# A two-block float32 kernel on one core: earlier gelu and gate loads, narrow weight fetches, recurrence banks in the other order, aligned input rows

## The reference

```
x = first_block(x):                       # hybrid_layer, then rmsnorm
    z = rmsnorm(x) @ w_in                 # 7 parts of 1024 columns
    a recurrence over the tokens per head: r, i = sigmoid(block_diag(rnn_x)), h = a*h + u
    x += merged @ w_out; x += (silu(g)*u) @ w_down; x += gate * (p @ w_ple)
y = second_block(x):                      # hybrid_layer_2
    proj = rmsnorm(x) @ w_in_2            # 11 parts: queries, keys, values, gates, low-rank parts
    o_a = nsa_mixer(...)                  # compressed, selected and window attention
          compress: gelu(blk @ w1) @ w2   # over blocks of 32 tokens, 31 blocks
    o_b = mla_mixer(...)
    h = x + concat(rmsnorm(o_a), rmsnorm(o_b)) @ w_out
    return h + peer_ffn(rmsnorm(h))       # 16 of 128*128 experts for each of 8 heads:
          a = x . expert_u[e]; y = sum(gate * gelu(a) * expert_v[e])
```

## Time and profile before

| | |
|---|---|
| timed runs | 2511.75, 2513.43, 2515.58 us; median 2513.43 |
| profiled execution | 2519.97 us, of which the span from first to last instruction 2518.2 us |
| busy, share of the span | PE 97%, PE weight load 85%, DVE 67%, POOL 44%, ACT 34% |
| mean granted clock of PE | 0.992 of 2.4 GHz |
| DMA | 517.06 MB, 205 GB/s over the span; over 90% busy in the last third |
| weight fetches | 196 of 704 KB; 256 of 512 KB for u and v units |

### The profile page before, as it was taken

The page is one execution under the profiler, slowest core; times in us unless marked ns, Lnnn a source line. Parts: engine busy times, 40 slices in busy tenths (PEclk is TensorE's granted clock), DMA queues, the critical chain, the costliest instruction groups (busy, mean ns, idle before and its releaser), DMA issues.

```text
span 2518.2 us, 36877 instructions
## 1 busy us (share of the span) xinstructions
PE 2443.1 (97%) x13021; PEld 2147.7 (85%) x13021; DVE 1698.5 (67%) x2879; ACT 859.6 (34%) x1497; POOL 1097.1 (44%) x671
## 2 busy tenths in 40 slices
PE   6999999999999999899899999999999999999999
PEld 5777877888887888555688999999999899999999
DVE  6767675463433642776744699888886678787877
ACT  3333222100113314676323333344443333333332
POOL 4666666665664541000463688841112333333231
PEclk9999999999999998999999999999999999999999
DMA  4444434433433324000232699999999999999995
GB/s 157 138 138 137 138 115 150 137 106 114 137 105 114 115 93 161 1 1 1 81 126 97 215 316 308 305 334 342 345 341 370 383 340 336 345 348 338 345 340 198
DMA packets 181334, 517.06 MB, mean 205 GB/s; under 512 B 14848, under 2 KB 80512, under 8 KB 181248
## 3 DMA queue, kind: packets, MB, share of 16 engines
q1 hardware_dynamic: 144384, 381.76, 45.2%
q0 software_dynamic: 36864, 134.23, 14.1%
HBM read 463.50 MB, written 52.43 MB: 205 GB/s over the span
## 4 chain that ended last, share of the span: by engine, by line
PE 88%; issue 4%; POOL 3%; DVE 2%; ACT 1%; DMA 1%; SPq 0%; DVEq 0%; ACTq 0%; POOLq 0%
PE ps L589 38%; PE ps L1091 37%; POOL spl L2264 2%; PE ps L1025 2%; PE ps L1112 2%; PE ps L681 1%; PE ps L988 1%; PE ps L1002 1%; DVE st L1944 1%; POOL rare L2274 1%; PE ps L947 1%; PE ps L780 1%; PE ps L742 1%; PE ps L984 1%; DMA gelu<-gst 1%
## 5 line engine op out<-in xcount | busy, mean ns | idle before, releaser
L589 PE MATMUL ps<-hh,spl 128*128 128x512 f32 x1840 | 573.6, 392 | 14.6 <-DVE hl L1982 6.4
L1091 PE MATMUL ps<-wsp,spl 128*128 128x384 f32 x3072 | 541.8, 337 | 5.5 <-DVE wsp L2156 4.7
L1091 PEld LDWEIGHTS ps<-wsp,spl 128*128 128x128 f32 x3072 | 532.5, 188 | 13.0 <-DVE wsp L2156 10.2
L1091 PE MATMUL ps<-hh,spl 128*128 128x384 f32 x2048 | 535.3, 337 | 2.8 <-POOL spl L2264 2.7
L1454 ACT ACTIVATE spl<-ring 128x1024 fp32r<-128x1024 f32 x256 | 271.7, 1061 | 704.5 <-PE ps L1091 681.3
L2199 POOL CAST spl<-ring 128x1024 fp32r<-128x1024 f32 (+1 forms) x167 | 187.2, 1121 | 660.1 <-PE ps L589 562.3
L2201 POOL TENSOR_TENSOR spl<-ring,spl 128x1024 fp32r<-128x1024 f32 (+1 forms) x167 | 435.6, 2609 | 13.4
L589 PEld LDWEIGHTS ps<-hh,spl 128*128 128x128 f32 x1840 | 347.4, 189 | 94.3 <-issue 10.9
L1091 PEld LDWEIGHTS ps<-hh,spl 128*128 128x128 f32 x2048 | 371.2, 188 | 5.9 <-issue 5.3
L589 PE MATMUL ps<-hl,spl 128*128 128x512 f32 x920 | 359.7, 391 | 0.0
L1091 PE MATMUL ps<-hl,spl 128*128 128x384 f32 x1024 | 342.5, 334 | 0.0
(11 more groups left out here) (381 smaller groups left out, 3248.5 us busy)
## 6 DMA issues: line engine op xcount, KB each, us to landing
ring<-stream_in SPq DMA_DIRECT2D x196, 704.0 KB
ring<-u_in SPq DMA_DIRECT2D x128, 512.0 KB
ring<-v_in SPq DMA_DIRECT2D x128, 512.0 KB
gelu<-gst SPq DMA_DIRECT2D x128, 192.0 KB
dense<-stage SPq DMA_DIRECT2D x12, 2048.0 KB
gl<-gelu SPq DMA_DIRECT2D x32, 768.0 KB, 6.8
gw<-dense SPq DMA_DIRECT2D x32, 768.0 KB, 9.2
x<-x_in SPq DMA_DIRECT2D x4, 512.0 KB, 6.3
```

Of the source, the lines that this page charges most:

```text
L589: m = pe.matmul(ps[:, bank, :], w[:, part, k0 + k * n:k0 + k * n + P], rhs(k), start=first and k == 0 and part == 0 and rhs is high, stop= ...
L1091: m = pe.matmul(ps[:, bank, 0:TD], w[:, part, k0 + k * P:k0 + (k + 1) * P], rhs(k), start=first and k == 0 and part == 0 and rhs is high, ...
```

## The change

1. The three first quads (`quad(0, 0)` to `quad(0, 2)`) are issued behind the fetches and saves at u units 123, 125 and 127, instead of behind v units 0, 1 and 2. The waits for `g_stored` and the first four `gelu_saved` of each go with the first.
2. SP fetches only the first 1024 columns of a unit (512 KB), except for units 76 to 135 (1408, by the loop) and 156, 157 (1120). Units 136 to 195 are no longer a loop but 60 unrolled fetches.
3. In `recurrence` results o = 0, 1 go to banks 6 + o instead of 7 - o; the wait for `z_evac` stands ahead of o = 0; chunk 6 waits for three of the four evacuations.
4. `sqc_end` grows from 8 to 128 bytes on each partition. With the 32-byte steps of the allocation `il2`, `mqr`, `rt` and `ih` move up by 96 bytes.

```diff
-        sb("sqc_end", [P, 2], c=pre)
+        sb("sqc_end", [P, 32], c=pre)
...
-                sp_.dma_start(ring[:, s, :], stream[s, :, :]).then_inc(w_ready[s], 16)
-            def unit_load(i, s):
+                sp_.dma_start(ring[:, s, 0:D], stream[s, :, 0:D]).then_inc(w_ready[s], 16)
+            def unit_load(i, s, n):
 
                 sp_.wait_ge(unit_done, i * RING + (s + 1))
-                sp_.dma_start(ring[:, s, :], stream[bass.ds(i * RING + (RING + s), 1), :, :]
+                sp_.dma_start(ring[:, s, 0:n], stream[bass.ds(i * RING + (RING + s), 1), :, 0:n]
                               .rearrange("a p n -> p (a n)")).then_inc(w_ready[s], 16)
 
             with sp_.Fori(0, U_FF // RING) as i:
                 for s in range(RING):
-                    unit_load(i, s)
+                    unit_load(i, s, D)
...
-            with sp_.Fori(U_FF // RING, N_UNITS // RING - 1) as i:
+            with sp_.Fori(U_FF // RING, U_PLE // RING) as i:
                 for s in range(RING):
-                    unit_load(i, s)
-            for u in range(N_UNITS // RING * RING, N_UNITS):
+                    unit_load(i, s, UNIT)
+            for u in range(U_PLE + RING, N_UNITS):
+                n = 4 * VW if U_TOK <= u < N_SPLIT else D
                 sp_.wait_ge(unit_done, u - RING + 1)
-                sp_.dma_start(ring[:, u % RING, :], stream[u, :, :]).then_inc(w_ready[u % RING], 16)
+                sp_.dma_start(ring[:, u % RING, 0:n], stream[u, :, 0:n]).then_inc(w_ready[u % RING], 16)
...
+            early = 0
             for i in range(U_PLAIN // 4 + 2 + SLABS, N_KEYS // 4):
                 for j in range(RING):
                     u_load(i, j)
                     save_late(i, j)
-            for k in range(2):
-                sp_.wait_ge(g_stored[k], 16 + 16 * ((SLABS + 1 - k) // 2))
-            for j in range(4):
-                sp_.wait_ge(gelu_saved[j], 16 + 16 * 4)
+                    if N_KEYS - 4 * i - j in (5, 3, 1):
+                        if early == 0:
+                            for k in range(2):
+                                sp_.wait_ge(g_stored[k], 16 + 16 * ((SLABS + 1 - k) // 2))
+                            for k in range(4):
+                                sp_.wait_ge(gelu_saved[k], 16 + 16 * 4)
+                        quad(0, early)
+                        early += 1
             for j in range(RING):
                 v_load(0, j)
                 save_late(N_KEYS // 4, j)
-                if j < 3:
-                    quad(0, j)
...
                         pe.wait_ge(rg_evac, i * 4 + (2 * g + o + 1))
-                        if g == 0 and o:
+                        if g == 0 and o == 0:
                             pe.wait_ge(z_evac, i * 14 + Z_BANKS)
                         for kk in range(2):
-                            m = pe.matmul(ps[:, 7 - o, :], w[:, (2 * kk + o) * P:(2 * kk + o + 1) * P],
+                            m = pe.matmul(ps[:, 6 + o, :], w[:, (2 * kk + o) * P:(2 * kk + o + 1) * P],
                                           xc[:, kk, :], start=kk == 0, stop=kk == 1)
...
-                        pe.wait_ge(rg_evac, i * 4 + 2 + 4)
+                        pe.wait_ge(rg_evac, i * 4 + 2 + 3)
...
-                                eng.activation(dst[:, o, :], ps[:, 7 - o, :], ACT.Sigmoid, bias=pd(b, i * 2 + o))\
+                                eng.activation(dst[:, o, :], ps[:, 6 + o, :], ACT.Sigmoid, bias=pd(b, i * 2 + o))\
```

## The result

| | kernel before | kernel after |
|---|---|---|
| median of the timed runs | 2513.32 us (4 runs, 2511.75 to 2515.58) | 2499.45 us (4 runs, 2499.34 to 2500.38) |
| profiled execution | 2519.97 us, span 2518.2 | 2499.37 us, span 2497.6 |
| mean granted clock of the profiled execution | 0.992 | 0.998 |

The ratio is 0.9945, interval 0.9928 to 0.9962: 13.9 us faster where 19.5 were forecast. The two profiled executions differ by 20.6 us. Executions of one and the same kernel differ in where the clock falls to half: 63 later runs of the kernel before lay between 2512.8 and 2522.5 us, with mean granted clocks of 0.995 down to 0.991.

What follows compares the result with a forecast made beforehand. TensorE was taken to bound the kernel (88% of the chain), so only its waits and slowed matmuls counted. 6.7 + 3.3 + 8.2 + 1.3 = 19.5 us off the median 2513.43 gave 2494 us, range 2490 to 2506.

Steps and rivals of the forecast that it cites:

- Boundary, 6.7 us: From u to v units: last save lands 4.4 us sooner, plus 2.3 us of clock; bounds 2.2 to 7.0.
- C: At the boundary the save lands only 2.2 us sooner; a 2.5 us wait with clock fall stays: 2498.5; chance 0.10.
- D: Both the half clock at L947 and a boundary wait with its clock fall remain: 2506.7; chance 0.12.
- E: Slower: the three early gelu and gate pairs delay the u units and PE waits: 2516; chance 0.05.
- Recurrence, 3.3 us: Turned bank order removes PE's wait for ACT's evacuation in four heads, 4 x 0.84 us; bounds 2.5 to 3.4.
- Narrow fetches, 8.2 us: Compression products, L947: fetch wait 0.86 us and half clock there and at L813, 5.64 + 1.74; bounds 0 to 8.2.
- about 14.5: Sign of being right: the 128 matmuls of L947 take about 14.5 us.
- rival B's first half: The half clock at L947 stays, the 0.86 us wait not being its cause: 2502; chance 0.28 for both halves.
- Alignment, 1.3 us: Matmuls reading `ih` come every 227.7 instead of 231.7 ns if the address is the reason; bounds 0 to 1.3.
- I take the same sum off both: Whole kernel: 19.5 us off the profiled execution (to about 2500.5) and off the timed median (to 2494).
- rival B's second half: The half clock at L947 wasn't in the timed runs before the change: 2502; chance 0.28 for both halves.

Runs made afterwards that it cites:

- x10_filler: The kernel before with 8 more products ahead of the wait for unit 165 at L947, fetches still 704 KB: 2512.27 us, ratio 0.9980.
- x7_cmp_narrow: The kernel before with 512 KB instead of 704 KB fetches for the compression products' units 161 to 168 alone: 2514.39 us, ratio 0.9982.
- x8_cmp_wide: The kernel after with units 165 to 168 fetched at 704 KB again: 2506.98 us, beside 2499.80 for the unchanged kernel after.

## Why the prediction was right in direction and too large in size

**Boundary, 6.7 us.** The mechanism is as forecast, and so is the gain in the profile, 6.7 us. The size of one step was wrong, how much sooner SP's queue is through. I took the idle DMA time from the busy share (2.2 us, so 4.4 us sooner); the earlier trace rows have GB/s beside it, and against 415 the stretches from 1940 to 1950 lack 74 and 246 GB/s, 1.6 MB, and with half of 415 for SP's queue 7.7 us. Measured: 7.4. It changed little, because 4.7 us of wait is all there is to win. Measured alone: 4.8 (2.5 to 7.1). The fetches of the u units weren't late: no wait of PE between units 123 and 127. Rivals C, D and E are out.

**Recurrence, 3.3 us.** The mechanism is right, the size too small: each head is 1.1 us shorter and not 0.84, 4.3 us in the profile, above the bound of 3.4, and 4.5 (2.5 to 6.8) in the timed runs. The term held only the idle time; 0.26 us a head lay in the products behind it.

**Narrow fetches, 8.2 us.** The cause was right: the wait sets off the stretch at half clock; with the wait filled or removed the stretch is gone, and with the wait put back it is there again (`x10_filler`, `x7_cmp_narrow`, `x8_cmp_wide`). 128 products take 14.24 us against "about 14.5". The size was too large: 5.5 us in the profile. At the old place the gain was even 9.1 us, as the products of L954 and L960 behind L947 had run at half clock too (1.84 us, now 1.01) and the term left them out. What I didn't ask is who is late next when PE comes through 7 us earlier. It was POOL's subtraction, which in the kernel before was over 2 us ahead of DVE's L1929 and now runs beside it; 1.9 us of wait came back, and in the profile of the kernel after 1.6 us of clock loss behind it: 9.1 - 1.9 - 1.6 = 5.6. I asked what is late next for the boundary and the recurrence, and not here.
On the rule of the Trainium skill that I weighed ("TensorE: Matmul & The Clock Gate", "Why this matters for your kernels", long idle gaps): here 0.6 to 1.0 us between short products were enough, while four waits of 0.85 us in the mixer brought no fall. The measurement decides: rival B's first half is out.

**Alignment, 1.3 us.** The address is a reason, but for 1.6 of the 4.0 ns: 0.5 us. The products on `ih` and on `acth` differ in something else too, which wasn't looked for.

**From the sum to the timed median.** This is the step that failed most. "I take the same sum off both" was applied to a profiled execution with 41 us at half clock and to a median of three runs 6.5 us shorter. The sum held 2.3 + 5.64 + 1.74 = 9.7 us of clock, which can be won only in executions in which the clock falls there. The time of a profiled execution was forecast at 2500.5 and came at 2499.37, and that is in part luck: where something was changed the two profiles differ by some 16 us, and 4.2 us come from clock falls elsewhere. The median came at 2499.45 and not at 2494.

Whether the stretch at L947 was missing from those timed runs, rival B's second half, isn't settled, as their clock isn't on record. The five profiles that have the wait all have the stretch. But one of the six timed runs of `x8_cmp_wide` took 2500.7 us at a mean clock of 0.997, which is what the kernel after does without the stretch. So it may be missing from a run.

Over many runs the account closes to about 2 us. The 63 runs of before have a mean clock of 0.9927 and a mean span of 2516.2 us, 14 runs of the kernel after 0.9970 and 2498.9, which is 17.3 us less. By the clock 0.0073 x 2516 = 18.4 us were lost against 0.0030 x 2499 = 7.5, a gain of 10.9 if PE works all through these stretches, so at most that. To it come the waits that are gone, 4.7 + 3.3 + 0.9, less the new 1.9, together 7.0; 1.0 for the 0.26 us a head; 0.5 for the alignment. That is 19.4 us at most. So the 19.5 that were forecast are near what many runs give, with a recurrence that gives more and a compression stage that gives less than its term.

That it was 13.9 the first time lies in four runs of the kernel before at the low end of its spread, 2515.6 us and less; of the 63 later runs eight are that low. So chance alone is an unlikely reason, and what it was stays open.

## What to carry to other kernels

Price a wait of TensorE by its idle time and by the clock behind it, and look at the clock of each stretch before believing a sum: where the clock loss is in the profiled run but not surely in the timed ones, take it off the profiled time only. Behind some waits the fall came in every profile, behind others in most: several profiles of one kernel tell which. When a stage gets shorter, ask for each engine what now runs beside what; here POOL and DVE met, and a wait of 1.9 us took the place of one of 0.9. Room on the DMA engines was better read here from GB/s against the full rate (7.7 us, measured 7.4) than from the busy share (4.4).

## What the runs showed of the hardware that was not expected

- A wait of 0.6 to 1.0 us among products of 62 columns is followed by 13.7 to 17.1 us at half clock, in five profiles of five; eight filler products in the gap keep the clock full.
- The same 2.7 us wait in the same code is followed by a fall to half in one execution and by none in the next; ten of twelve profiles have the fall.
- With the recurrence's results in the other order of banks a head gains not only the wait of 0.85 us but 0.26 us more in the 336 products behind it.
- A DVE product of 0.25 us with both operands in SBUF took 2.26 us behind a POOL subtraction that had started 0.2 us earlier, and 1.71 us behind one that had started 0.8 us earlier: so short an operation can cost PE 1.9 us.
- Moving operands that start on a multiple of 128 bytes save about 1.6 ns of 232 per product of 512 columns, against a start 96 bytes lower.
